# A new order of the steps in the sparse and the stick-breaking stage of a 16-stage block kernel

## The reference, cut to what is computed

```python
def stick_breaking_attention(h, w_in, w_out):          # 8 heads of 128
    q, k, v = split(h @ w_in, 3)
    z = q @ k.T * scale
    log_beta = log_sigmoid(z)
    log_fail = where(earlier, log_beta - z, 0.0)
    log_a = log_beta + cumsum(log_fail, reverse=True) - log_fail
    return (where(earlier, exp(log_a), 0.0) @ v) @ w_out

def dsa_sparse_attention(h, w_in, cq_g, ckv_g, kidx_g, w_uq, w_qidx, w_uk, w_uv, w_out):
    proj = h @ w_in                                    # 384 + 256 + 32 + 64 + 8 columns
    c_q, c_kv = rmsnorm(proj[:384], cq_g), rmsnorm(proj[384:640], ckv_g)
    k_rope = rope(proj[640:672]); k_idx = partial_rope(rmsnorm(proj[672:736], kidx_g))
    q = c_q @ w_uq                                     # 8 heads, the first 32 of 128 roped
    q_idx = partial_rope(c_q @ w_qidx)                 # 8 index heads of 64
    score = sum_h(w_idx[h] * relu(q_idx[h] @ k_idx.T)) # causal
    idx = top_k(score, 64)
    ...                                                # attention over the chosen keys alone
    return o @ w_out
```

## Time and profile before

| | |
|---|---|
| median of 3 runs | 2943.78 us (2941.07 to 2945.3) |
| span of the profiled execution | 2946.0 us |
| TensorE matmul busy | 2891.8 us, 98% |
| VectorE, ScalarE, GpSimd busy | 1813.9, 1598.2, 417.1 us |
| stick-breaking stage | about 754 to 864 us |
| sparse stage | about 1232 to 1333 us |

### The profile page before, as it was taken

One profiled execution on the slowest core, in us unless ns is written; L12 is line 12 of the kernel. 1 busy time (PEld: TensorE's weight loads), 2 busy tenths in 40 slices (PEclk: granted clock), 3 DMA queues, 4 the chain that ended last, 5 costly groups with the idle time before them and its releaser, 6 DMA issues.

```text
span 2946.0 us, 36491 instructions
## 1 busy us (share of the span) xinstructions
PE 2891.8 (98%) x14543; PEld 2451.5 (83%) x14543; DVE 1813.9 (62%) x2192; ACT 1598.2 (54%) x2013; POOL 417.1 (14%) x636
## 2 busy tenths in 40 slices
PE   9999999999999999989999999999999999999998
PEld 7888888888988888878888888888888888888887
DVE  6568566555666556465556486555665765675664
ACT  5447754444464454565444377644565563566562
POOL 1203212021002112041202115021000020000020
PEclk9999999999999999999999999999999999999999
DMA  8754168676548677537768643376645596645694
GB/s 276 239 188 142 45 194 245 196 236 219 182 147 246 214 219 236 180 99 219 231 202 242 200 149 124 93 239 225 190 153 176 197 281 213 198 147 180 211 278 156
DMA packets 397050, 575.08 MB, mean 195 GB/s; under 512 B 20016, under 2 KB 248624, under 8 KB 396880
## 3 DMA queue, kind: packets, MB, share of 16 engines
q1 hardware_dynamic: 372624, 508.75, 54.9%
q0 software_dynamic: 23680, 62.95, 6.9%
q10 hardware_dynamic: 576, 1.05, 0.1%
HBM read 540.16 MB, written 32.51 MB: 194 GB/s over the span
## 4 chain that ended last, share of the span: by engine, by line
PE 85%; DVE 7%; ACT 5%; issue 1%; DMA 1%; POOL 0%; SPq 0%; DVEq 0%; ACTq 0%; POOLq 0%
PE ps L430 25%; PE ps L432 25%; PE ps L431 25%; PE ps L616 3%; DVE lo L656 2%; ACT hi L638 1%; DVE qkv L1641 1%; PE ps L503 1%; PE ps L505 1%; PE ps L504 1%; ACT sl L1416 1%; ACT qkv L1416 1%; PE ps L603 0%; PE ps L587 0%; DMA raw<-in_ffn_w_gu 0%
## 5 line engine op out<-in xcount | busy, mean ns | idle before, releaser
L656 DVE TENSOR_TENSOR lo<-raw,hi 128x2048 fp32r<-128x2048 f32 (+3 forms) x473 | 1057.5, 2246 | 654.0 <-ACT hi L638 653.4
L638 ACT ACTIVATE hi<-raw 128x2048 fp32r<-128x2048 f32 (+2 forms) x487 | 906.8, 1870 | 725.2 <-DMA raw<-in_ffn_w_gu 285.7
L430 PE MATMUL ps<-hi,xh 128*128 128x512 f32 (+1 forms) x2208 | 865.0, 392 | 5.5 <-DVE lo L656 2.3
L432 PE MATMUL ps<-hi,xl 128*128 128x512 f32 (+1 forms) x2208 | 858.0, 389 | 0.0
L431 PE MATMUL ps<-lo,xh 128*128 128x512 f32 (+1 forms) x2208 | 857.4, 388 | 0.0
L430 PEld LDWEIGHTS ps<-hi,xh 128*128 128x128 f32 x2208 | 414.6, 188 | 91.8 <-DVE lo L656 5.3
L432 PEld LDWEIGHTS ps<-hi,xl 128*128 128x128 f32 x2208 | 414.4, 188 | 86.1
L431 PEld LDWEIGHTS ps<-lo,xh 128*128 128x128 f32 x2208 | 414.8, 188 | 82.7
L430 PE MATMUL ps<-hi,hhh 128*128 128x512 f32 x704 | 274.6, 390 | 0.0
L432 PE MATMUL ps<-hi,hhl 128*128 128x512 f32 x704 | 274.0, 389 | 0.0
L431 PE MATMUL ps<-lo,hhh 128*128 128x512 f32 x704 | 273.9, 389 | 0.0
(11 more groups left out here) (443 smaller groups left out, 3405.0 us busy)
## 6 DMA issues: line engine op xcount, KB each, us to landing
raw<-in_ffn_w_gu SPq DMA_DIRECT2D x348, 512.0 KB, 4.8
raw<-in_ffn_w_down SPq DMA_DIRECT2D x80, 1024.0 KB, 5.3
raw<-in_w_ff SPq DMA_DIRECT2D x64, 1024.0 KB, 6.0
raw<-in_w_in SPq DMA_DIRECT2D x60, 1024.0 KB, 5.3
raw<-in_gdn_w_in SPq DMA_DIRECT2D x32, 1024.0 KB, 5.8
turned<-hhf POOLq DMA_DIRECT2D x88, 256.0 KB, 4.9
hhr<-turned POOLq DMA_DIRECT2D x352, 64.0 KB, 4.4
raw<-in_sb_w_in SPq DMA_DIRECT2D x12, 1024.0 KB, 5.1
```

The costliest lines, as they stand in the source:

```text
L430: e.matmul(o, a1, r1, start=kk == 0, stop=False)
L432: i = e.matmul(o, a2, r1, start=False, stop=kk == kts - 1)
L638: k.e.activation(k.m.hi[q % RING][:, 0:n], k.m.raw[q % RING][:, 0:n], ACT.Copy).then_inc(*k.up("act_piece_hi", ("hi", q)))
L656: k.e.tensor_tensor(m.lo[i][:, 0:n], m.raw[i][:, 0:n], m.hi[i][:, 0:n].bitcast(F32), ALU.subtract).then_inc(*k.up("dve_piece_lo", ("split" ...
```

## The change

Only the scripts change: 3 of the stick-breaking stage and 4 of the sparse stage. Every lane still issues the same portions in the same order among themselves; what changes is how lanes are interleaved on each engine. One line of two of the tables:

```diff
 DSA_ACT = """
-W x1 W W W p0 W W normq W W normq W p1 W normq W W normk normk qi index_q normk normk W W index_q uq W normk turn_q
+W turn_q W x1 W W p0 normq normq W W W W W turn_q W index_q turn_q normq p1 normk normk W normk W qi uq index_q W W W
 DSA_DVE = """
-W x1 W W W W W normq W W normq W W normq W W normk normk index_q normk normk W W index_q W normk turn_q turn_q index
+normq x1 W W W W normq W normk W W W normq W normk W W W normk normk index_q normk turn_q turn_q turn_q index index_q
```

More of the change, by code:

```diff
@@ L1851 @@
 SB_PE = """
-W x1 rbc W W W W rbc W W W W W W heads W heads W heads W heads W heads W heads W heads W W W heads heads heads W heads
-W heads W heads W heads heads heads W heads heads heads heads W heads W W W next W W W
+W rbc x1 W W W W W W rbc W W W W heads W W heads heads heads W W heads W W heads heads W heads W W heads heads W heads
+W heads heads W heads heads W heads W heads heads heads heads W heads W W W next W W W
 """
 SB_ACT = """
-W x1 rbc W W W W rbc W W W W W W heads W heads W heads W heads W heads W heads W heads W W v W heads heads heads W
-heads W heads W heads v W heads heads heads W heads heads heads heads W heads W W W next W W W
+W W x1 rbc W W W W rbc W W W W W heads W heads W W heads heads heads W heads W W W heads W heads W v heads heads W
+heads heads heads heads heads heads W v W heads W heads heads W heads W W heads next W W W W W
 """
 SB_DVE = """
-W x1 rbc W E W W W E rbc E W E W W W E W W heads W heads W heads W E heads W E heads E W heads W heads W W W heads
-heads heads W heads W heads W heads W heads heads heads W heads heads heads heads W heads W out W W next W W W out out
+x1 W W W W rbc W E E W W W W E E W E heads W heads heads E W W heads heads heads E W W heads W heads W W E W heads
+heads heads heads W heads heads heads heads heads W W heads heads heads W heads out W W W next W W out W out W W W rbc
 """
@@ L2179 @@
 DSA_PE = """
-W x1 W W W W W normq W W normq W W normq W W normk normk index_q normk normk W W index_q W normk turn_q turn_q index
-turn_q index index index W index index W W index turn_q W index turn_k index attention attention attention attention
-attention attention W attention attention W attention attention attention attention W W W next W W W
+normq turn_q W index_q x1 W W W normk W W normq W W normq W W W turn_q normk W normk W turn_q W W normk normk index_q
+index W index index index turn_q W W W turn_k attention attention attention attention attention attention attention W
@@ L2183 @@
+attention index attention index index W index attention attention W attention W index W W next W W
 """
 DSA_ACT = """
-W x1 W W W p0 W W normq W W normq W p1 W normq W W normk normk qi index_q normk normk W W index_q uq W normk turn_q
-turn_q index turn_q index index index W index index uv W W index uk turn_q W index turn_k index attention attention
-attention attention attention attention W attention attention W attention attention attention attention W W W next W W
-W
+W turn_q W x1 W W p0 normq normq W W W W W turn_q W index_q turn_q normq p1 normk normk W normk W qi uq index_q W W W
@@ L2189 @@
+W index normk W index index index index index W uv turn_q uk turn_k attention attention attention W attention
+attention attention W attention W attention attention attention W attention attention normk W W W W index index index
+next W
 """
 DSA_DVE = """
-W x1 W W W W W normq W W normq W W normq W W normk normk index_q normk normk W W index_q W normk turn_q turn_q index
-turn_q index index index W index index W W index turn_q W index index attention attention attention attention
-attention attention W attention attention W attention attention attention attention W out W W next out W W W out
+normq x1 W W W W normq W normk W W W normq W normk W W W normk normk index_q normk turn_q turn_q turn_q index index_q
@@ L2194 @@
+index index index W index W index index index index attention attention W attention W W attention attention turn_q
+attention attention attention W W attention attention attention W attention W out W W W out next out W W W
 """
 DSA_POOL = """
-W W W W W W W W W W W W W W W W W W W attention attention attention attention attention attention W attention
-attention W attention attention attention attention W W W W W W
+W W W W attention W W W W W W W W W W W W W W attention attention attention W attention attention attention attention
@@ L2198 @@
+attention W attention W W W W W W attention W attention
 """
```

## The result

The changed kernel takes 2950.8 us (12 runs, 2949.3 to 2952.5), the kernel before 2944.6 us in runs beside it (12 runs, 2941.1 to 2947.0). The ratio is 1.0022, with a 95% interval of 1.0015 to 1.0030: 4.4 to 8.8 us slower, 6.2 by the medians. The forecast was 2945.0; the time lies 0.3 us above the end of the range, and it is the time of rival B.

What follows compares the result with a forecast made beforehand. TensorE, 98% busy, was taken as the bound. A later mask (+1.9), attention (-1.5) and 0 to 1.7 us of clock, taken together as +1.2 on 2943.8, gave 2945 us; range 2938.5 to 2950.5.

Steps and rivals of the forecast that it cites:

- rival B: After scoring, GpSimd's o3 subtraction goes before VectorE's masking additions; top-64 4.6 us later, 2949 to 2950.5 us; chance 0.25.
- The hand-over behind the split of uk: Between scoring and top-64, VectorE's masking addition goes before GpSimd's waiting o3 subtraction and takes 0.3 us.
- The clock of qi: In the q projection on TensorE: full clock instead of mostly 1.2 GHz, which had cost 2.9 us.
- the base: Whole kernel: the profiled execution's 2.2 us over the median carries over unchanged, so the sum starts from 2943.8 us.
- rival D: Something in the stick-breaking stage or at a stage's end loses its cover, 1 to 6 us: 2947 to 2951; chance 0.10.
- The stick-breaking stage: Its edits change nothing, as TensorE has no idle time there: 0, with 0 to +1 us as bounds.
- The idle time before qi: On TensorE ahead of the q projection: 0.5 us and not 2.77 us, with the norm of q moved ahead.
- The three high parts and the first ReLU: ScalarE's splits of uk, o1, o2 precede the first ReLU, at 1267.2 against 1267.75; 0.5 of 4.9 us lead left.
- the two subtractions against the chain: GpSimd's o1 and o2 subtractions block VectorE's scoring, the second for 4.6 us; scoring ends at 1279.9.
- Top-64 and mask: On VectorE from the end of scoring, split of uk aside, to the mask: 11.6 us.
- From attention to w_out: From attention's start to VectorE's sum of w_out's first half: 27.8 us against 29.3, a gain of 1.5 us.
- The idle time behind index head 5: TensorE idles over 6 us in one piece during index scoring, costing 0 to 1.7 us of clock.

Runs made afterwards that it cites:

- uk_early: The changed kernel with the low part of uk on VectorE made ahead of the index scores again; 2946.1 us, ratio to the kernel before 1.0009.
- o3_late: The changed kernel with ScalarE's high part of o3 moved behind the copies of the turned q; 2946.2 us, ratio to the kernel before 1.0009.
- before_again: The kernel before, unchanged, profiled once more; 2941.3 us in one run.
- o2_late: The changed kernel with ScalarE's high part of o2 behind the last ReLU again, ahead of that of o3; 2950.6 us, ratio to the kernel before 1.0023.

## Why the prediction was wrong, point by point

**The hand-over behind the split of uk: the wrong step.** The forecast gave the port to VectorE's masking additions and took 0.3 us for them, on the strength of the instruction at 251.58 in the earlier trace rows. The first of them took 4.69 us. This is rival B, as the prediction described it, to the place and to 0.1 us. With the addition freed and all else left (uk_early, o3_late) attention starts 3.5 to 3.6 us earlier and the time falls by 3.5 us; the rest of the 4.4 us was covered by TensorE's own work. The row at 4.62 us in the earlier trace rows was the nearer one: there a subtraction of the same size held an instruction of the same stage, behind another of VectorE's. Why the instruction at 251.58 went ahead of GpSimd stays open; it does so again, at the same durations (0.68 us, and 3.63 us on GpSimd), in the second profile of before and in that of the changed kernel.

**The clock of qi and the base: the second wrong step.** The forecast took 2.9 us of clock as a gain, and carried the profiled execution over "as it is". That execution was an unusual one: it has 3.3 us more up to the first ReLU than before_again, 31.2 against 27.9. Of these, 1.3 us are the later start of qi behind the late transfer of uq1, and 2.0 us the half clock in qi (2.5 us) less a wait of 0.5 us behind qi that came back in before_again. Device times lie 1.85 us above the span of the same execution (2951.75 and 2949.9 in the changed kernel's), so it stood 4 us above the median of the three runs, not 2.2. Against the second profile of before the ReLUs are not 0.5 us earlier but 2.1 us later. That rival B's range, 2949 to 2950.5, came so close to 2950.8 is partly luck, since two errors cancel. Against the first profile w_out comes 3.6 us later (87.8 less 84.1) and not B's 5.0, mostly because scoring ended 0.7 us earlier than in the sum and top-64 and mask took 0.3 us less; and the base was off the other way: the profile stood 1.9 us further above the median than the sum took, and the rise on the medians is larger by that.

**The ledger against before_again.** To the first ReLU +2.1 us (30.0 less 27.9: the lead of the norm, less two more high parts). First ReLU to the end of scoring +1.4 us (12.6 against 11.2). End of scoring to attention +5.1 us (17.5 against 12.4): split 1.7, held addition 4.4, less 0.5 that VectorE had been waiting for TensorE, 0.3 for which a GpSimd subtraction had held a mask instruction (L2469, 0.54 us there and 0.22 us here), and 0.1 between the pieces. Sum 8.6 us. Attention to w_out -2.1 us (27.6 against 29.8). In all 6.5 us. The medians say 6.2, but the spans of these two executions differ by 10.4 us: 0.5 us lie ahead of the landmark and 3.4 us behind w_out. The way from w_out to the end takes 1622.2 to 1626.8 us over all twelve profiles, and TensorE waits for nothing from 1330 to 1400 us in either kernel, so nothing shows that the end of the stage lost its cover (rival D); what the 3.4 us are is not shown. The ledger says where the stretch lost its time, and its nearness to the medians is partly luck.

**What held.** The stick-breaking stage at nothing. The idle time before qi gone, qi ended at 1249.8 (forecast 1250.2). The three high parts and the first ReLU at 1266.5 (1267.2). The forecast for the two subtractions against the chain: one scoring instruction between them, scoring over at 1279.2 (1279.9). Top-64 and mask: 11.1 us behind the held addition, 11.3 us with an addition of usual length (11.6; the mask instruction that was held before makes the difference). From attention to w_out 27.6 us, and 28.8 us in the second profile (27.8). The idle time behind index head 5 and half clock behind it.

**The chances.** B had 0.25 against 0.45 for the forecast, from one row each way, and its upper end took no account of the base. o2_late shows that the part with the most weight, who waits at the moment of the hand-over, could be read from the order: each subtraction that stands ready costs the next VectorE instruction that it can hold 4.6 us.

## What to carry to other kernels

A GpSimd instruction of several us that becomes ready while VectorE is in a long instruction costs the next short one on VectorE nearly its whole length in each case of this stage (the instruction at 251.58, in another stage, is the exception), so list what stands ready on GpSimd at each point of a VectorE chain, and let it fall on instructions that it doesn't hold or on idle time. Split work goes behind the chain that ends last, not ahead of it: with the ReLUs ahead of the high parts, the same kernel came out level with the one before, and with o2 and o3 moved once more 0.15% faster, instead of 0.22% slower. And before a clock that one profile shows is counted as a gain, compare that execution's span with those of the other runs, take a second profile, and see whether a transfer landed late in the first.

## What the runs showed of the hardware

- Turns in the sparse stage: behind a held VectorE instruction, or behind a split, GpSimd's waiting subtraction went next. One VectorE instruction at a time was let in between two subtractions (L2448, 2.57 and 4.60 us; L2455 and L2456, 4.63 and 4.68 us). In the first recurrent stage it was the other way once: a GpSimd product that had waited through a split let one more VectorE instruction go ahead (3.63 us on GpSimd, 0.68 us on VectorE).
- Instructions with one tensor in SBUF are held as well: L2448 (128x256) and L2470 (128x128), both TENSOR_SCALAR in float32, for 4.6 us. The rounds of top-8 (MAX8, MATCH_REPLACE8) ran beside a subtraction of 4.60 us at their usual length (0.62 us for two MAX8 in uk_early, 0.61 us in the changed kernel with no subtraction beside them). The Trainium skill ("SBUF — State Buffer", Who interferes with whom) counts tensor_scalar among the operations that can take the shared ports; the trace agrees, with 4.59 us.
- Idle time and clock: behind 1.06 and 1.71 us of idle time with six transposes between them, the 18 matmuls of qi ran at a granted clock of 0.54; behind 1.7 us alone they ran at 1.00, in three profiles. Whether the second wait made the difference isn't known from these runs.
- A transfer of 1024 KB took 7.0 us from issue to landing in one execution, and 5.0 to 5.3 us at the same place in three others.
